# A hybrid decoder step on one core: the sample rows' last tile laid over 128 partitions, and two steps of the ending reordered

## The chip, the cores and the metric

The kernel runs on one core of a Trainium2 chip. The metric is the device time in microseconds of one execution of the whole program, as the median of several runs; a profile of one execution gives the trace that is read here.

## What is computed

One layer of a decoder for 512 prompt rows and 64 sample rows of 1024 values (D), all in float32. The layer is a sum of three gated branches (a state space scan, windowed attention, attention into memory tokens), and then a mixture of experts over all 576 rows. Only its last part matters for this change:

```python
x = x + merged @ lp['w_out']                                  # h
x = x + hier_moe(rmsnorm(x, lp['norm2_g']), lp)               # y = h + w0 * expert_a(x) + w1 * expert_b(x)
...
def rmsnorm(x, g):
    xf = x * lax.rsqrt(jnp.mean(x * x, axis=-1, keepdims=True) + EPS)
    return xf * g
```

Each row goes through two of 32 experts. Its result is h plus the two experts' rows, each times a weight, and the final RMSNorm is taken of that sum with the gain `final_norm_g`.

## The kernel before, in words

The 576 rows lie as five tiles. `WROWS = [64, 128, 128, 128, 128]` and `WTOK = [512, 0, 128, 256, 384]` say that tile 0 holds the 64 sample rows (512 to 575) on 64 partitions, and tiles 1 to 4 hold 128 prompt rows each. Each tile has h in SBUF at `H_AT[t]` as rows of 1024 columns.

The experts' stage runs over 16 pairs of experts (`pairs`). Its weights come in 96 chunks of 1 MB on SyncE's DMA queue (L567), and they are what the stage waits for. The experts' result rows are scattered to a DRAM tensor `expert_rows` by GpSimd (L2929), pair by pair. The last pair's result isn't scattered: it is picked out of PSUM by matmuls with one-hot matrices (`picked`, L1338), after it was split into a high and a low half in fp32r (`L_HI` and `L_LO`, written at L1881 and L2742).

SyncE sets the loads' order around the end (L603 to L617). When the last pair's rows are turned, it issues `load_gain` (L604: the gain, one DRAM row of 4 KB sent to all 128 partitions), which stands in the DMA queue behind the experts' last weights. It then waits for the scatters and issues `load_results` (L609), five loads of `expert_rows` in the order `LOADED = [1, 3, 4, 2, 0]`, 1 MB for each full tile and 512 KB for tile 0.

The ending is written out by hand, the same for TensorE, ScalarE, VectorE and SyncE:

- VectorE adds the first expert's rows to h (`add_first`, L2732), and for tiles 1, 3 and 4 puts that sum plus the second expert's rows into PSUM (`seed`, L2737). Tile 2 gets its second expert's rows in `combine` (L2789), which reads TensorE's sum from PSUM and writes to SBUF. `finish` (L2799, L2800) takes the reciprocal of the root and scales the sum by it and by the gain.
- TensorE (`sums`, L1367) writes a zero first matmul into each seeded PSUM pair (`opening`), adds h of tiles 0 and 2 (`own_rows`), adds the last pair's rows (`picked`), and for tiles 2 and 0 also the loaded rows times their weights (`rows_of`). PSUM holds tile 3's sum in pair ps0, tile 1's and then tile 4's in ps1, tile 2's in ps2 and tile 0's in ps3.
- ScalarE (L1886 to L1893) squares each sum with an accumulated row sum, and takes the root of it.
- SyncE (L634 to L637) stores each finished tile to `out_y`.

```python
ORDER = [1, 3, 2, 0, 4]          # finish and store
...
seed(1); seed(3); add_first(4)
finish(1)
finish(3)
combine(2)
seed(4)
finish(2)
finish(0)
finish(4)
```

(The calls stand one below the other from L2802 to L2811.) Semaphore `more_ps` counts the finished sums in PSUM, `rootf` the roots, `y_done` the finished tiles, `opened` and `seeded` the seeded tiles. The profile's lines L667 and L681 are the helpers through which every matmul and transpose goes.

## Time and profile before

| | |
|---|---|
| median of 3 runs | 781.47 us (778.28 to 782.59) |
| the profiled execution's own time | 779.59 us |
| its span, first to last instruction | 777.8 us |
| granted TensorE clock, mean | 0.993 of full speed |
| busy: TensorE matmul / VectorE / ScalarE / GpSimd | 95% / 53% / 33% / 10% of the span |
| DMA, mean over the span | 245 GB/s |
| last VectorE instruction begins, its length | 771.83 us, 1.28 us |

The profiled execution's own time is 1.79 us longer than its span: what lies around the first and last instruction. Starts in the rows are microseconds from the span's start, so the change's place, the ending, is the stretch from some 728 us on. "Idle before, releaser" says how long an engine stood still before an instruction and what ended that. Time from issue to landing is that of one DMA, from its issue until its semaphore shows it complete.

### The profile page before, as it was taken

What the parts mean: (1) busy time and instruction counts of PE and PEld (TensorE: products, weight loads), DVE (VectorE), ACT (ScalarE), POOL (GpSimd) and SP (SyncE); (2) the same over time, 40 slices, a digit from 0 to 9 for tenths busy, and PEclk for the clock granted to TensorE, in tenths of its full rate; (3) what the DMA queues carried; (4) which work ended last, traced back from release to release, by engine and by line L of the source; (5) the groups of instructions that cost most, each with busy time, mean ns of one, the idle gap of its engine ahead of it and who ended that gap; (6) DMA issues with size and microseconds to landing.
All of it is one profiled execution on the core that took longest, in us unless ns stands there. A gap on an engine that the chain in (4) does not pass through costs nothing.

```text
span 777.8 us, 12795 instructions
## 1 busy us (share of the span) xinstructions
PE 736.3 (95%) x5298; PEld 568.6 (73%) x5298; DVE 409.2 (53%) x756; ACT 260.4 (33%) x451; POOL 74.7 (10%) x105
## 2 busy tenths in 40 slices
PE   8999999999999999999999999998899999778784
PEld 6999999999999777899999988884333333323232
DVE  6999839986347785666154286555121111114226
ACT  5662361123486645443342333230111111100113
POOL 0100022001002111000000100011112212111100
PEclk9999999999999999999999999999999999999998
DMA  9678226434238442500251596389999999999995
GB/s 343 214 271 311 103 82 107 118 116 149 105 120 309 173 158 95 208 1 2 109 184 47 188 413 248 99 354 392 406 422 423 419 423 424 420 425 424 422 395 190
DMA packets 38191, 190.78 MB, mean 245 GB/s; under 512 B 5930, under 2 KB 7498, under 8 KB 21912
## 3 DMA queue, kind: packets, MB, share of 16 engines
q1 hardware_dynamic: 23696, 148.22, 48.3%
q0 software_dynamic: 11248, 35.08, 13.5%
q10 hardware_dynamic: 3184, 6.60, 2.3%
q8 instruction: 44, 0.72, 0.4%
q14 instruction: 19, 0.16, 0.0%
HBM read 176.27 MB, written 21.41 MB: 254 GB/s over the span
## 4 chain that ended last, share of the span: by engine, by line
PE 75%; DMA 15%; DVE 5%; ACT 3%; issue 1%; SPq 1%; ACTq 0%; DVEq 0%; POOLq 0%
PE ps L667 71%; DMA sb<-in_wexp 11%; PE ps L681 4%; DMA expert_rows<-sb 2%; DMA sb<-in_xT 1%; DMA sb<-expert_rows 1%; DVE sb L2800 1%; DVE sb L2330 1%; DVE sb L2316 1%; SPq L567 1%; ACT sb L1455 1%; ACT sb L1655 1%; DVE sb L2732 0%; ACT sb L1677 0%; ACT sb L1660 0%
## 5 line engine op out<-in xcount | busy, mean ns | idle before, releaser
L667 PE MATMUL ps<-sr 128*128 128x288 f32 (+3 forms) x2906 | 407.5, 300 | 2.7 <-DVE ps L2737 2.3
L667 PEld LDWEIGHTS ps<-sr 128*128 128x128 f32 (+1 forms) x2906 | 386.8, 188 | 18.3 <-issue 5.8
L667 PE MATMUL ps<-sb 128*64 128x512 f32 (+17 forms) x1994 | 292.2, 427 | 27.0 <-DMA sb<-in_wexp 15.0
L667 PEld LDWEIGHTS ps<-sb 128*64 128x64 f32 (+7 forms) x1994 | 141.9, 145 | 149.8 <-issue 123.0
L2666 DVE SCALAR_TENSOR_TENSOR sb<-sb,ps 128x256 f32<-128x256 f32 x16 | 6.7, 421 | 116.2 <-ACT sb L1860 116.2
L681 PEld LDWEIGHTS ps<-sb 128*128 128x128 f32 (+3 forms) x398 | 42.2, 140 | 32.6 <-issue 30.2
L681 PE MATMUL ps<-sb 128*128 128x128 f32 (+3 forms) x398 | 53.8, 273 | 3.8 <-DVE sb L2669 1.6
L2278 DVE TENSOR_TENSOR sr<-sb,sr 128x2048 fp32r<-128x2048 f32 (+1 forms) x17 | 39.3, 2319 | 29.0 <-ACT sr L1569 19.0
L2674 DVE COPY sb<-ps 128x1024 f32<-128x1024 f32 x15 | 18.4, 1225 | 57.2 <-PE ps L667 57.2
L1455 ACT ACTIVATE sb<-ps 128x576 f32<-128x576 f32 (+4 forms) x33 | 23.2, 704 | 71.8 <-PE ps L667 56.0
L2389 DVE SCALAR_TENSOR_TENSOR sb<-sb,ps 128x576 f32<-128x576 f32 x24 | 18.1, 752 | 46.5 <-PE ps L667 46.3
L1855 ACT ACTIVATE sb<-ps 128x256 f32<-128x256 f32 x16 | 6.1, 384 | 97.2 <-PE ps L681 97.2
L1860 ACT ACTIVATE sb<-ps 128x256 f32<-128x256 f32 x16 | 6.1, 384 | 78.4 <-PE ps L667 78.4
L1569 ACT ACTIVATE sr<-sb 128x2048 fp32r<-128x2048 f32 x16 | 30.5, 1914 | 1.9 <-ACT sb L1716 0.9
L2929 POOL DMA_INDIRECT expert_rows<-sb x15 | 15.1, 1008 | 154.3 <-DVE sb L2674 139.5
L1716 ACT ACTIVATE sb<-ps 128x288 f32<-128x288 f32 x24 | 9.7, 410 | 54.2 <-PE ps L667 53.8
L2236 DVE TENSOR_TENSOR sr<-sb,sr 128x2048 fp32r<-128x2048 f32 x7 | 16.0, 2292 | 22.5 <-ACT sr L1574 16.6
L2033 DVE TENSOR_TENSOR sr<-sb,sr 128x2048 fp32r<-128x2048 f32 x10 | 22.8, 2292 | 2.3 <-ACT sr L1477 2.0
L1655 ACT ACTIVATE sb<-sb 128x256 f32<-128x256 f32 (+2 forms) x36 | 16.6, 463 | 18.5 <-DVE sb L2333 18.5
L1477 ACT ACTIVATE sr<-sb 128x2048 fp32r<-128x2048 f32 x10 | 19.0, 1911 | 5.1 <-DVE sb L2101 4.5
L1850 ACT ACTIVATE sb<-ps 128x1024 f32<-128x1024 f32 x15 | 15.4, 1024 | 15.3 <-PE ps L681 15.3
L2920 POOL DMA_INDIRECT sb<-xn_rows,sb x15 | 15.3, 1019 | 31.6 <-issue 12.6
(293 smaller groups left out, 499.7 us busy)
## 6 DMA issues: line engine op xcount, KB each, us to landing
sb<-in_wexp SPq DMA_DIRECT2D x91, 1024.0 KB, 21.4
sb<-in_wstream SPq DMA_DIRECT2D x33, 1024.0 KB, 5.5
expert_rows<-sb ACTq DMA_DIRECT2D x1, 4608.0 KB, 24.8
sb<-in_mkT POOLq DMA_DIRECT2D x8, 512.0 KB, 7.9
sb<-in_mv POOLq DMA_DIRECT2D x8, 512.0 KB, 5.3
sb<-expert_rows SPq DMA_DIRECT2D x4, 1024.0 KB, 9.0
sb<-in_wexp SPq DMA_DIRECT2D x5, 768.0 KB, 21.6
sb<-in_x SPq DMA_DIRECT2D x4, 512.0 KB, 14.0
```

The costliest lines, as they stand in the source:

```text
L667: return signed(nc.tensor.matmul(*a, **kw))
L681: return signed(nc.tensor.transpose(*a))
L1455: c.free(fn(dst, src, ACT.Copy, **kw), job)
L1477: fn(r32(EARLY_HI[b], WB), at(raw_at(b), (1, WB)), ACT.Copy).then_inc(hi_ready, 1)
L1569: fn(r32(high_at(block), 2048), at(raw_at(b), (1, WB)), ACT.Copy).then_inc(hi_ready, 1)
L1655: fn(at(sc + m * 256, (1, keys)), at(sc + m * 256, (1, keys)), ACT.Exp, bias=at(stat(n, 1) + m, (1, 1)), accum_out=at(stat(n, 3) + m, (1, 1)))
L1850: fn(at(M_XGT, (1, 1024)), pat(PS_X, 0, (1, 1024)), ACT.Copy).then_inc(xT_sb, 1)
L2033: v.tensor_tensor(r32(raw_at(b), WB), at(raw_at(b), (1, WB)), r32(EARLY_HI[b], WB).bitcast(F32), ALU.subtract).then_inc(lo_ready, 1)
L2236: v.tensor_tensor(r32(src, 2048), at(src, (1, 2048)), r32(hi, 2048).bitcast(F32), ALU.subtract).then_inc(lo_ready, 1)
L2278: v.tensor_tensor(r32(src, n), at(src, (1, n)), r32(hi, n).bitcast(F32), ALU.subtract).then_inc(lo_ready, 1)
L2389: c.free(v.scalar_tensor_tensor(g2, g2, 1.0, pat(pair(name), 0, (512, 2), (1, TH)), ALU.add, ALU.mult), name)
L2674: v.tensor_copy(at(M_YO + (i % 2) * 1024, (1, 1024)), pat(PS_Y, 0, (1, 1024))).then_inc(y_copied, 1)
```

## The change

Tile 0's sum lies in PSUM as 128 partitions by 512 columns now: columns 0 to 511 of its 64 rows on partitions 0 to 63, and columns 512 to 1023 on partitions 64 to 127 (`half_sum`). What reads or writes it follows:

- `own_rows(0)` and `rows_of(0)` write each half to its own 64 partitions. `picked(0)` writes 128 partitions at once, with a one-hot matrix that is moved by 64 places for the second half; for that `L_SEL` has 704 columns instead of 640, and `pick_slots` one small instruction more.
- ScalarE squares 128x512 instead of 64x1024. A row's sum of squares then lies in two parts on partitions p and p+64, which a one-column matmul with the matrix `L_PAIR` adds (`both_squares`); `L_PAIR` is made by one new VectorE instruction in `weight_diagonals`. The root of tile 0 is taken from PSUM, after tile 4's.
- `load_gain` loads the gain a second time in that layout, by two DMAs of 64 partitions by 512 columns to `L_GF`.
- Tile 0 is stored by two DMAs of 64x512.

The order changes too. Tile 0 is squared before tile 4 as before, but finished and stored after it: `ORDER = [1, 3, 2, 4, 0]`. On VectorE `combine(2)` and `seed(4)` stand ahead of `finish(3)`. On TensorE `rows_of(2)` stands ahead of `picked(0)`.

```diff
-ORDER = [1, 3, 2, 0, 4]
+ORDER = [1, 3, 2, 4, 0]
+L_PAIR, L_GF = 46624, O_XH
...
             def load_gain():
                 sp.dma_start(at(M_GF, (1, D)), bass.AP(rows.tensor, rows.offset + D, [[0, P], [1, D]])).then_inc(ld["gf"], 16)
+                for half in range(2):
+                    sp.dma_start(at(L_GF, (1, 512), p0=64 * half, pn=64),
+                                 bass.AP(rows.tensor, rows.offset + D + half * 512, [[0, 64], [1, 512]])).then_inc(ld["gf"], 16)
...
+                if t == 0:
+                    for half in range(2):
+                        sp.dma_start(out_y[WTOK[t]:WTOK[t] + R, half * 512:half * 512 + 512],
+                                     at(H_AT[t], (1, 512), p0=64 * half, pn=64)).then_inc(y_st, 16)
...
+            def half_sum(t, half):
+
+                if t == 0:
+                    return pat(PICKED[t], 0, (1, 512), p0=64 * half, pn=64)
+                return pat(PICKED[t], half * 512, (1, 512), pn=WROWS[t])
...
-                        last = mm(pat(PICKED[t], half * 512, (1, 512), pn=R), r32(L_SEL + WTOK[t], R),
+                        out = pat(PICKED[0], 0, (1, 512)) if t == 0 else half_sum(t, half)
+                        last = mm(out, r32(L_SEL + WTOK[t] + (64 * half if t == 0 else 0), P),
                                   r32(y + half * 512, 512), start=False, stop=(stop and k == 1))
...
+            def both_squares():
+
+                pe.wait_ge(squares, 2 * TT + 3 + 3)
+                mm(pat(PICKED[0], 512, (1, 1)), at(L_PAIR, (1, 128)), at(R_SS + 8, (1, 1)), start=True, stop=True).then_inc(more_ps, 1)
...
                 picked_on_seed(3)
-                picked(0)
                 pe.wait_ge(diag_w, 2)
                 rows_of(2, R_DG)
+                picked(0)
                 pe.wait_ge(y_done, 1)
                 opening(4)
                 rows_of(0, R_BOTH)
                 picked_on_seed(4)
+                both_squares()
...
+            for n, t in enumerate((1, 3, 2)):
+                final_square(n, t)
+                final_root(t)
+            final_square(3, 0)
+            final_square(4, 4)
+            final_root(4)
+            act.wait_ge(more_ps, TT + 1)
+            final_root(0)
...
             def finish(t):
-                R = WROWS[t]
-                h, ss = at(H_AT[t], (1, D), pn=R), at(R_SS + 8 + t, (1, 1), pn=R)
-                total = h if t == 2 else pat(PICKED[t], 0, (1, D), pn=R)
+                n, gf = (512, L_GF) if t == 0 else (D, M_GF)
+                h, ss = at(H_AT[t], (1, n)), at(R_SS + 8 + t, (1, 1))
+                total = h if t == 2 else pat(PICKED[t], 0, (1, n))
...
             finish(1)
-            finish(3)
             combine(2)
             seed(4)
+            finish(3)
             finish(2)
+            finish(4)
             finish(0)
-            finish(4)
```

How the instructions stand, first TensorE's end of `sums`, before. Names with `sr` are fp32r, with `sb` float32; the four `sr` rows of one tile are a `picked`, two `sr` rows with `y_done` are `opening(4)`, and the `sb` rows are `rows_of`.

```order
L667 MATMUL ps<-sr 128x512 [waits seeded]
L667 MATMUL ps<-sr 128x512 x3
L667 MATMUL ps<-sr 64x512 x4
L667 MATMUL ps<-sb 128x512 [waits ld_row2,diag_w]
L667 MATMUL ps<-sb 128x512
L667 MATMUL ps<-sr 128x512 [waits y_done]
L667 MATMUL ps<-sr 128x512
L667 MATMUL ps<-sb 64x512 [waits ld_row0]
L667 MATMUL ps<-sb 64x512
L667 MATMUL ps<-sr 128x512 [waits seeded]
L667 MATMUL ps<-sr 128x512 x3
```

And the same place in the changed kernel:

```order
L676 MATMUL ps<-sr 128x512 [waits seeded]
L676 MATMUL ps<-sr 128x512 x3
L676 MATMUL ps<-sb 128x512 [waits ld_row2,diag_w]
L676 MATMUL ps<-sb 128x512
L676 MATMUL ps<-sr 128x512 x4
L676 MATMUL ps<-sr 128x512 [waits y_done]
L676 MATMUL ps<-sr 128x512
L676 MATMUL ps<-sb 64x512 [waits ld_row0]
L676 MATMUL ps<-sb 64x512
L676 MATMUL ps<-sr 128x512 [waits seeded]
L676 MATMUL ps<-sr 128x512 x3
L676 MATMUL ps<-sb 128x1 [waits squares]
```

The four matmuls of `picked(0)` moved behind `rows_of(2)`, and a one-column matmul came at the end.

VectorE from the first `finish` on, before (L2799 and L2800 are `finish`, L2789 is `combine(2)`, L2737 is `seed(4)`):

```order
L2800 SCALAR_TENSOR_TENSOR sb<-ps,sb 128x1024 [waits vec_step]
L2799 RECIPROCAL sb<-sb 128x1 [waits rootf]
L2800 SCALAR_TENSOR_TENSOR sb<-ps,sb 128x1024 [waits vec_step]
L2789 SCALAR_TENSOR_TENSOR sb<-sb,ps 128x1024 [waits more_ps,ld_row2]
L2737 SCALAR_TENSOR_TENSOR ps<-sb 128x1024 [waits opened]
L2799 RECIPROCAL sb<-sb 128x1 [waits rootf]
L2800 SCALAR_TENSOR_TENSOR sb<-sb 128x1024 [waits vec_step]
L2799 RECIPROCAL sb<-sb 64x1 [waits rootf]
L2800 SCALAR_TENSOR_TENSOR sb<-ps,sb 64x1024 [waits vec_step]
L2799 RECIPROCAL sb<-sb 128x1 [waits rootf]
L2800 SCALAR_TENSOR_TENSOR sb<-ps,sb 128x1024 [waits vec_step]
```

And in the changed kernel:

```order
L2837 SCALAR_TENSOR_TENSOR sb<-ps,sb 128x1024 [waits vec_step]
L2826 SCALAR_TENSOR_TENSOR sb<-sb,ps 128x1024 [waits more_ps,ld_row2]
L2774 SCALAR_TENSOR_TENSOR ps<-sb 128x1024 [waits opened]
L2836 RECIPROCAL sb<-sb 128x1 [waits rootf]
L2837 SCALAR_TENSOR_TENSOR sb<-ps,sb 128x1024 [waits vec_step]
L2836 RECIPROCAL sb<-sb 128x1 [waits rootf]
L2837 SCALAR_TENSOR_TENSOR sb<-sb 128x1024 [waits vec_step]
L2836 RECIPROCAL sb<-sb 128x1 [waits rootf]
L2837 SCALAR_TENSOR_TENSOR sb<-ps,sb 128x1024 [waits vec_step]
L2836 RECIPROCAL sb<-sb 128x1 [waits rootf]
L2837 SCALAR_TENSOR_TENSOR sb<-ps,sb 128x512 [waits vec_step]
```

`combine(2)` and `seed(4)` moved ahead of the second `finish`, and the last instruction works on 512 columns instead of 1024.

SyncE's queue in the changed kernel, from the gain's load on:

```order
L605 DMA sb<-in_rows 128x1024 [waits xt_ps]
L607 DMA sb<-in_rows 64x512 x2
L613 DMA sb<-expert_rows 128x2048 [waits ew_used,y_sent1,y_sent0]
L613 DMA sb<-expert_rows 128x2048 x3
L613 DMA sb<-expert_rows 128x1024
L622 UNCONDITIONAL_BRANCH
L646 DMA out_y<-sb 128x1024 [waits y_done] x4
L643 DMA out_y<-sb 64x512 [waits y_done]
L643 DMA out_y<-sb 64x512
```

The two loads at L607 are new and stand between the gain and the result rows; the last store is two of 64x512 where a 128x1024 one was last.

## Rows read from the trace of the kernel before

**Rows 1.** The page: DMA share in 40 slices of the span; chain shares by engine.
```profile
DMA  9678226434238442500251596389999999999995
...
PE 75%; DMA 15%; DVE 5%; ACT 3%; issue 1%; SPq 1%; ACTq 0%; DVEq 0%; POOLq 0%
```

**Rows 2.** The chain that ended last, 730 to 778 us: start, us, what.
```profile
748.50 5.96 DMA sb<-expert_rows
...
754.49 1.30 DVE sb L2732
...
771.83 1.28 DVE sb L2800
```

**Rows 3.** SyncE's queue in order of time: start, us spent issuing, line, count.
```profile
727.96 1.41 SPq L604 DMA_DIRECT2D sb<-in_rows  x1
748.50 2.62 SPq L609 DMA_DIRECT2D sb<-expert_rows  x5
...
773.14 0.34 SPq L637 DMA_DIRECT2D out_y<-sb  x1
```

**Rows 4.** DMA issues in windows around them: count, KB each, us to landing.
```profile
sb<-in_rows SPq DMA_DIRECT2D x1, 512.0 KB, 24.0
...
sb<-expert_rows SPq DMA_DIRECT2D x1, 1024.0 KB, 6.0
...
sb<-expert_rows SPq DMA_DIRECT2D x1, 1024.0 KB, 12.1
...
out_y<-sb SPq DMA_DIRECT2D x1, 512.0 KB, 2.6
...
out_y<-sb SPq DMA_DIRECT2D x1, 512.0 KB, 4.2
```

**Rows 5.** Packets of a queue in five windows: 62-66, 749.2-749.8, 765.6-768.3, 772.7-774.0, 751.0-751.6.
```profile
q10 hardware_dynamic: 799, 1.64, 104.9%
...
q1 hardware_dynamic: 29, 0.16, 131.9%
...
q1 hardware_dynamic: 275, 1.05, 96.4%
...
q1 hardware_dynamic: 61, 0.25, 90.6%
...
DMA packets 35, 0.26 MB, mean 430 GB/s; under 512 B 2, under 2 KB 2, under 8 KB 5
```

**Rows 6.** Timeline of the ending, VectorE.
```profile
755.81 1.41 DVE L2742 SCALAR_TENSOR_TENSOR sr<-ps,sb,sr 128x512 fp32r<-128x512 f32 x2
...
764.84 1.28 DVE L2800 SCALAR_TENSOR_TENSOR sb<-ps,sb 128x1024 f32<-128x1024 f32 x1
...
766.04 1.27 DVE L2789 SCALAR_TENSOR_TENSOR sb<-sb,ps 128x1024 f32<-128x1024 f32 x1
...
767.23 1.28 DVE L2737 SCALAR_TENSOR_TENSOR ps<-sb 128x1024 f32<-128x1024 f32 x1
...
770.44 1.27 DVE L2800 SCALAR_TENSOR_TENSOR sb<-ps,sb 64x1024 f32<-64x1024 f32 x1
```

**Rows 7.** Timeline of the ending, TensorE; fp32 matmuls leave two records each.
```profile
753.75 1.03 PE L667 MATMUL ps<-sb 128*64 128x512 f32 x4
...
763.63 1.88 PE L667 MATMUL ps<-sb 128*128 128x512 f32 x4
764.94 1.03 PE L667 MATMUL ps<-sr 128*128 128x512 f32 x2
765.90 1.93 PE L667 MATMUL ps<-sb 128*64 128x512 f32 x4
768.57 1.19 PE L667 MATMUL ps<-sr 128*128 128x512 f32 x4 [0.74 <-DVE ps L2737]
```

**Rows 8.** Timeline of the ending, ScalarE: tile 4's square and root.
```profile
770.06 1.00 ACT L1891 ACTIVATE sb<-ps 128x1024 f32<-128x1024 f32 x1
...
771.19 0.29 ACT L1893 ACTIVATE sb<-sb 128x1 f32<-128x1 f32 x1
```

More of the change, by code:

```diff
@@ L1283, in own_rows @@
                 for half in range(2):
-                    mm(pat(PICKED[t], half * 512, (1, 512), pn=R), at(O_ID, (1, R), pn=R),
+                    mm(half_sum(t, half), at(O_ID, (1, R), pn=R),
                        at(H_AT[t] + half * 512, (1, 512), pn=R), start=start, stop=not start)
@@ L1362, in rows_of @@
                 for half in range(2):
-                    last = mm(pat(PICKED[t], half * 512, (1, 512), pn=R), at(weights, (1, R)), at(A_WG[t] + half * 512, (1, 512)),
+                    last = mm(half_sum(t, half), at(weights, (1, R)), at(A_WG[t] + half * 512, (1, 512)),
                               start=False, stop=True)
                 last.then_inc(more_ps, 1)
+            def both_squares():
+                pe.wait_ge(squares, 2 * TT + 3 + 3)
+                mm(pat(PICKED[0], 512, (1, 1)), at(L_PAIR, (1, 128)), at(R_SS + 8, (1, 1)), start=True, stop=True).then_inc(more_ps, 1)
             def sums():
@@ L1885, in _, with final_square, final_root @@
             fn(at(R_SS + 15, (1, 1)), at(O_EPS, (1, 1)), ACT.Sqrt)
-            for n, t in enumerate(ORDER):
-                R = WROWS[t]
-                ss = at(R_SS + 8 + t, (1, 1), pn=R)
+            def final_square(n, t):
+                n_p, n_d = (P, 512) if t == 0 else (WROWS[t], D)
                 act.wait_ge(*((y_sum, 1) if t == 2 else (more_ps, SUMMED.index(t) + 1)))
-                total = at(H_AT[t], (1, D), pn=R) if t == 2 else pat(PICKED[t], 0, (1, D), pn=R)
-                fn(at(M_JUNK, (1, D), pn=R), total, ACT.Square, accum_out=ss).then_inc(squares, 1)
+                total = at(H_AT[t], (1, D)) if t == 2 else pat(PICKED[t], 0, (1, n_d), pn=n_p)
+                fn(at(M_JUNK, (1, n_d), pn=n_p), total, ACT.Square, accum_out=at(R_SS + 8 + t, (1, 1), pn=n_p)).then_inc(squares, 1)
                 act.wait_ge(squares, 2 * TT + 3 + n)
-                fn(ss, ss, ACT.Sqrt, scale=1.0 / D, bias=at(O_EPS, (1, 1), pn=R)).then_inc(rootf, 1)
+            def final_root(t):
+                ss = at(R_SS + 8 + t, (1, 1))
+                total = pat(PICKED[t], 512, (1, 1)) if t == 0 else ss
+                fn(ss, total, ACT.Sqrt, scale=1.0 / D, bias=at(O_EPS, (1, 1))).then_inc(rootf, 1)
+            for n, t in enumerate((1, 3, 2)):
[6 more added lines that the diff above has]
+            final_root(0)
         @block.vector
@@ L2681, in weight_diagonals @@
                 c.settle()
+                op(v.tensor_tensor(at(L_PAIR, (64, 2), (1, 64)), at(O_ID, (0, 2), (1, 64)), at(O_ID + 64, (0, 2), (1, 64)), ALU.add))
                 dve.sem_inc(diag_w, 1)
@@ L2706, in pick_slots @@
                 op(v.tensor_copy(at(L_W + 1, (1, 1)), at(M_IDX + 32 + NPAIR - 1, (1, 1)).bitcast(U32)), False)
+                op(v.tensor_scalar(at(L_TMP + 10, (1, 1)), at(R_IOTA + 8, (1, 1)), -float(RB), None, ALU.mult), False)
                 op(v.tensor_scalar(at(L_TMP, (1, 10)), at(R_IOTA, (1, 10)), -float(RB), None, ALU.mult))
-                op(v.tensor_scalar(at(L_TMP, (1, 10)), at(L_TMP, (1, 10)), at(L_W + 1, (1, 1)), None, ALU.add))
+                op(v.tensor_scalar(at(L_TMP, (1, 11)), at(L_TMP, (1, 11)), at(L_W + 1, (1, 1)), None, ALU.add))
                 dve.wait_ge(xt_ps, NPAIR)
-                c.do(v.tensor_tensor(view(sr, L_SEL, ((RB, 10), (1, RB))), at(R_IOTA, (0, 10), (1, RB)),
-                                     at(L_TMP, (1, 10), (0, RB)), ALU.is_equal), slot_oh, 3)
+                c.do(v.tensor_tensor(view(sr, L_SEL, ((RB, 11), (1, RB))), at(R_IOTA, (0, 11), (1, RB)),
+                                     at(L_TMP, (1, 11), (0, RB)), ALU.is_equal), slot_oh, 3)
             def pairs(i0, i1):
@@ L2774, in _ @@
                 dve.wait_ge(y_sent[1], 16 * (NPAIR_ALL // 2))
-                for dst, n in ((L_HI, 1024), (L_LO, 1024), (L_SEL, 640)):
+                for dst, n in ((L_HI, 1024), (L_LO, 1024), (L_SEL, 704)):
                     v.memset(r32(dst, n).bitcast(F32), 0.0).then_inc(y_lo, 1)
-                dve.wait_ge(ld["gf"], 32)
+                dve.wait_ge(ld["gf"], 96)
                 for t in range(TT):
```

12 lines of the change are left out of this document (6 added, 6 removed).

## The prediction

> **What bounds the kernel now.** I read the page first. TensorE heads the chain with 75%, and the DMA engines are 90% busy or more through the last quarter of the program [rows 1]. The change touches neither the experts' matmuls nor their weights, so the question is what hangs on the ending. The chain of waits over the last 50 us says how the ending is strung: SyncE issues the result loads at 748.50, the first lands 5.96 us later, VectorE starts at 754.49, and from there it is nearly all VectorE up to its last `finish`, 771.83 to 773.11 [rows 2]. Thus two things set the end: when the first result rows land, and how long VectorE's row of seven-odd large instructions takes. Each costs about 1.28 us and follows the one before almost at once [rows 6]. Behind VectorE stands the last store: issued at 773.14 [rows 3], landed 4.2 us later [rows 4], and 777.8 is the end of the span.
>
> **The gain's extra loads: on the path.** SyncE issues `load_gain` at 727.96 [rows 3], and it lands 24.0 us later, at 752.0 [rows 4]. That is after the result loads were issued, and both use the same queue. A load is complete when its slowest DMA engine is done, and in the window from 751.0 to 751.6 there are still 3 packets (5 under 8 KB, 2 of them semaphore writes under 512 B) of the gain's 4 KB kind among the result loads' 8 KB ones [rows 5]. So the slowest engine goes from the gain straight to the first result rows, which land at 748.50 + 6.0 = 754.5, where VectorE waits for them [rows 2, 4]. What is put between the two is added on that engine. The change puts two loads of 64 rows of 2 KB there: 128 packets, 8 on each of 16 engines. The nearest 2 KB packets are those of the queue between 62 and 66 us: 799 packets took 104.9% of 16 engines for 4 us, 84 ns each [rows 5]. 8 x 84 ns = **+0.67 us**. The lower bound is 0, if the slowest engine were not the one that counts. The upper bound of the usual kind is twice the price, 1.35 us, from tile 0's store: 61 packets of 4 KB took 90.6% of 16 engines for 1.3 us, 309 ns each, where the 128-row stores' 256 packets took 96.4% for 2.7 us, 163 ns each [rows 5]. A transfer that touches only 64 partitions went at about half the rate. The upper end of all is 3.5 us, from the slow packets between 749.2 and 749.8: 29 in 131.9% of 0.6 us, 437 ns each, 8 x 437 = 3.5 [rows 5]. I take 0.67, because at 751 the late engine works nearly alone, and because the 2 KB rows are of the same queue kind.
>
> The Trainium skill, "DMA: Bandwidth & Descriptors", section "The descriptor swizzle", says that partitions 0 to 63 lie on the even eight of the 16 SBUF ports and 64 to 127 on the odd eight; its "Rules for kernel authors" say of two transfers to disjoint partition halves: "Don't bother — they serialize". That speaks against the halves here, and tile 0's store at half rate agrees. By that rule the extra loads would cost the 1.35.
>
> All later loads shift with the first, and VectorE's chain with them, so the rest is reckoned in the times of before.
>
> **VectorE's order: earlier by a little.** Before, `finish(3)` starts at 764.84 and `combine(2)` at 766.04 [rows 6]. In the change `combine(2)` can start when `finish(1)` is through, at 764.65 to 764.84, if tile 2's sum is there. The sum: `rows_of(2)` runs 763.63 for 1.88 [rows 7], and four picks go from ahead of it to behind; four such matmuls take 1.19 [rows 7], so it ends at 765.51 - 1.19 = 764.3. Tile 2's loaded rows land 12.1 us after an issue at about 749.8, at 761.9, in time [rows 4]. So `combine(2)` ends near 765.95. `seed(4)` needs `opening(4)`, which stands behind the moved picks: 764.3 + 1.19 + 0.5 to 1.03 [rows 7] = 766.0 to 766.5. That is a new wait of up to 0.6 us on VectorE; `finish(3)`, whose root is long done, is queued behind it, and ScalarE's square of tile 4 waits at its far end. `seed(4)` starts at 766.3 instead of 767.23 [rows 6], ends at 767.6, and the four picks end at 768.8.
>
> Meanwhile `rows_of(0)` runs on TensorE from 766.3. It takes 1.93 if its halves go one after the other, as now, and about 1.03 if they overlap, as four records to alternating halves of the columns do at 753.75 [rows 7]. That puts tile 0's sum at 767.3 to 768.2. The Trainium skill, "TensorEngine Tiling (Array Packing)", section "Key Properties", says that tiles of different columns run in parallel; by it the 1.03 would hold. ScalarE squares 512 columns, between half of 1.00 and all of it [rows 8], with the accumulator's read say 0.8, and is free for tile 4 at 768.2 to 769.0. Tile 4's square and root take 771.19 + 0.29 - 770.06 = 1.42 [rows 8]: the root is there at 770.3 to 770.8. `finish(4)` then runs 770.5 to 771.0 for 1.28, its end 771.8 to 772.3. Tile 0's root follows tile 4's by some 0.3 and is covered by `finish(4)`; the one-column matmul in `both_squares` is covered by tile 4's square. `finish(0)` on 512 columns takes 0.70 (1.41 for two of that size) instead of 1.27 [rows 6] and a reciprocal 0.1. VectorE ends at 772.6 to 773.05 against 773.11: **-0.3 us** (-0.55 to -0.05). It is less than the halved `finish` and the moved steps suggest, since tile 4's path through TensorE and ScalarE is late next.
>
> **The stores: the small gain is spent.** A 512 KB store lands 2.6 us after its issue when nothing is late [rows 4]; by that, before would have been complete at 773.14 + 2.6 = 775.75. Now tile 4's store is issued at about 772.05 and would land at 774.65. Tile 0's two are issued at 772.9 and, after one issue of 0.34 [rows 3], 773.2, so their packets queue behind tile 4's. Their 128 packets of 2 KB, each half on 64 partitions, I price at half the 309 ns of tile 0's 4 KB packets: 8 x 155 ns = 1.24 us [rows 5]. That gives 775.9: the -0.3 of VectorE is spent, and ending and stores together make **+0.15 us**, between -0.5 (2 KB packets at 84 ns, 0.67 instead of 1.24) and +0.4 (VectorE at its late bound). One thing more: the last store took 4.2 us where another of its size took 2.6 [rows 4]. That 1.6 us may stay or go; I keep it, and let its loss be part of the low end.
>
> **Costed at nothing.** The `L_PAIR` instruction, the larger `L_SEL` and the extra instruction in `pick_slots` run beside the last pairs of experts, under weights that keep the DMA engines busy at 90% or more [rows 1]; without that cover they would cost some 0.5 us. GpSimd's queue isn't passed.
>
> **The sum.** +0.67 + 0.15 = +0.8 us. Against the profiled execution: 779.6 + 0.8 = 780.4. That one stood 1.9 us under the median of 781.5. On the median: **782.3 us**. 0.5%, about what a measurement of this kernel can tell from no change, is 3.9 us.
>
> **The rivals.**
> - *The queue has room.* Engines that ended early have a gap between 748.5 and 750; if the extra packets fall into it and the late engine comes no later, +0.67 goes, the ending gains its 0.5, and with the 1.6 us of the last store gone it is -2.1: 779.4 us. For it: the DMA engines move less in that gap. Against it: the engine that is late at 751 has none. 0.25. Still within 0.5%.
> - *Slower.* The gain's halves are read from one DRAM row by all engines while the result loads start, and each packet takes what packets took at 749.2, 437 ns [rows 5]: +3.5, with +0.4 at the end, +3.9, 785.4 us. It decides from 0.43 us per packet on; the late engine's packets must be slow, and not the first ones of the others. 0.05.
> - *The reordering does nothing.* If tile 2's sum or `opening(4)` is later than reckoned by 0.6, VectorE ends at 773.2, and the stores come on top: two issues of 0.34 and 2.6 of landing less the smaller size give at most +0.4, in all +0.67 + 0.4 = +1.1, 782.6 us. 0.15.
> - *The scatter of runs.* Three runs of before lie 4.3 us apart, so a median may seem faster by over 3.9 without a cause: 0.04.
>
> **How the numbers follow.** The forecast has 0.51. Its own bounds are 781.5 - 0.5 and + 1.35 + 0.4, 781.0 to 783.2. The range takes in the first and third rival and half a microsecond of scatter, 778.9 to 784.0; only the slow rival and odd medians lie outside. Faster: 0.04. Slower: the slow rival and scatter, 0.06. Within 0.5%: 0.90.
>
> **What would show it.** In the changed profile the gain's two halves land after 752, and the first result load lands 6.5 to 7 us after its issue instead of 6.0; VectorE's first add begins that much later. From that add to VectorE's last instruction it is 0.1 to 0.6 us less than the 18.6 of before. `combine(2)` follows `finish(1)` without a wait, and `seed(4)` waits 0.2 to 0.6. The chain ends on VectorE and two stores, with the last landing about 2.6 us or more after its issue. I am wrong if the first load lands after 6.0 us again, or if VectorE's ending is more than 1 us shorter.

## The result: slower by 0.29%, and the profile after

| | before | after |
|---|---|---|
| median of the runs (before: all those made beside the change) | 780.71 us | 782.57 us (781.14 to 784.26, 22 runs) |
| ratio after / before | | 1.0029, 95% interval 1.0021 to 1.0036 |
| the profiled execution's own time; its span | 779.59; 777.8 us | 783.69; 781.8 us |
| granted TensorE clock, mean | 0.993 | 0.985 |
| first `add_first` begins | 754.49 us | 757.40 us |
| last VectorE instruction ends | 773.11 us | 777.63 us |

0.29% of 780.7 is 2.3 us. This text goes by the recorded ratios and their intervals; two medians divided by each other can differ from them by up to 0.07% (here 1.0024, 1.9 us). The forecast was +0.8 us (782.3 on the median, range 778.9 to 784.0), no change that can be told. The time is in the range and the difference is under 0.5%, but it is two to three times as large as forecast, and its interval excludes both no change and +0.8. So the question is which term was too small.

The page of after, DMA shares and the chain's shares, against [rows 1]:

```profile
DMA  9578326434238432500260595389999999999993
...
PE 79%; DMA 12%; DVE 5%; ACT 3%; issue 1%; SPq 0%; ACTq 0%; DVEq 0%
```

Nothing has moved there: the ending is 4% of the span. The chain of waits after, last 57 us (start, us, what), against [rows 2]:

```profile
725.85 26.68 DMA sb<-in_wexp
752.52 0.14 issue
752.66 6.57 PE ps L676 x16
...
763.99 7.14 PE ps L676 x18
...
771.16 1.30 DVE ps L2774
...
776.88 0.75 DVE sb L2837
```

Before, this chain went through the first result load. Here it goes through the experts' last weights, which are complete only at 752.5, and then through TensorE. SyncE's queue after (start, us spent issuing, line, count), against [rows 3]:

```profile
728.57 1.40 SPq L605 DMA_DIRECT2D sb<-in_rows  x1
730.01 2.31 SPq L607 DMA_DIRECT2D sb<-in_rows  x2
748.18 3.22 SPq L613 DMA_DIRECT2D sb<-expert_rows  x5
...
777.66 1.40 SPq L643 DMA_DIRECT2D out_y<-sb  x2
```

The two small loads cost SyncE 2.31 us of issuing, under cover of the weights. The result loads are issued no later than before, 748.18 against 748.50. Their landings after (KB each, median us from issue to landing), against [rows 4]:

```profile
sb<-in_rows SPq DMA_DIRECT2D x1, 512.0 KB, 22.0
sb<-in_rows SPq DMA_DIRECT2D x2, 128.0 KB, 22.7
...
sb<-expert_rows SPq DMA_DIRECT2D x4, 1024.0 KB, 12.2
```

VectorE's timeline after (start, us, line, tiles, count, idle before and what ended it), against [rows 6]:

```profile
757.40 1.28 DVE L2769 SCALAR_TENSOR_TENSOR sb<-sb 128x1024 f32<-128x1024 f32 x1 [6.80 <-DMA sb<-expert_rows]
...
759.97 0.75 DVE L2779 SCALAR_TENSOR_TENSOR sr<-ps,sb,sr 128x512 fp32r<-128x512 f32 x1 [0.50 <-ACT sr L1902]
...
766.95 1.28 DVE L2837 SCALAR_TENSOR_TENSOR sb<-ps,sb 128x1024 f32<-128x1024 f32 x1
769.84 1.28 DVE L2826 SCALAR_TENSOR_TENSOR sb<-sb,ps 128x1024 f32<-128x1024 f32 x1 [1.60 <-PE ps L676]
771.16 1.29 DVE L2774 SCALAR_TENSOR_TENSOR ps<-sb 128x1024 f32<-128x1024 f32 x1
...
776.88 0.75 DVE L2837 SCALAR_TENSOR_TENSOR sb<-ps,sb 128x512 f32<-128x512 f32 x1
```

Two things went another way than forecast. The first result load landed 757.40 - 748.18 = 9.2 us after its issue, not 6.5 to 7. And the stretch from that add to VectorE's end is 20.2 us, not 18.0 to 18.5, because VectorE waited 0.50 for ScalarE, which stood behind the last pair's matmuls, and `combine(2)` waited 1.60 for TensorE. The timeline of TensorE and the granted clock after tell why. First the timeline, one line of before and two of after, against [rows 7]:

```profile
751.13 3.65 PE L667 MATMUL ps<-sb 128*64 128x512 f32 x16 [0.47 <-ACT sb L1855]
```
```profile
752.66 6.55 PE L676 MATMUL ps<-sb 128*64 128x512 f32 x16 [1.55 <-DMA sb<-in_wexp]
...
766.93 2.80 PE L676 MATMUL ps<-sb 128*128 128x512 f32 x4
```

Then windows of after (us from:to, length, busy us and count of PE, PEld, DVE, ACT, POOL; granted clock; DMA share; GB/s):

```profile
750.00:751.00 1.00, 0.30 (x2) 0.20 (x2) 0.56 (x2) 0.00 (x0) 0.00 (x0) 1.00 0.90 250
751.00:752.00 1.00, 0.11 (x2) 0.00 (x0) 0.00 (x0) 0.38 (x1) 0.00 (x0) 0.86 1.10 281
752.00:753.00 1.00, 0.34 (x2) 0.32 (x4) 0.00 (x0) 0.00 (x0) 0.00 (x0) 0.50 0.97 281
...
766.00:768.00 2.00, 2.00 (x5) 1.21 (x4) 1.53 (x3) 1.46 (x4) 0.00 (x0) 0.50 0.00 0
```

The last pair's 16 matmuls took 6.55 us here, where the same 16 took 3.65 before, and `rows_of(2)` took 2.80 instead of 1.88 [rows 7], both at the granted clock of 0.50, which is the 1.2 GHz level. The second fall of the clock is in this execution alone of the three profiles of the changed kernel; the other two have 18.1 and 18.0 us for the same stretch (below). So the 20.2 isn't what the change does as a rule, and this profile, 1.1 us above its kernel's median, shows more than the median lost. The other thing is in the last two columns: from 750 to 753 the DMA engines are busy (0.90 to 1.10) and move only 250 to 281 GB/s. Before, one microsecond was as slow, from 749 on (229 GB/s at 0.96), and engines as busy moved 434 to 438 from 751 on:

```profile
751.00:752.00 1.00, 0.87 (x4) 0.34 (x6) 0.00 (x0) 0.07 (x1) 0.00 (x0) 1.00 1.04 438
752.00:753.00 1.00, 1.00 (x8) 0.39 (x6) 0.00 (x0) 0.00 (x0) 0.00 (x0) 1.00 1.04 434
```

A packet is the piece that one DMA engine moves at a time, here 2 to 8 KB of a row. The packets of the 6 us from 748 to 754, before and after (packets, MB, share of 16 engines):

```profile
q1 hardware_dynamic: 331, 2.08, 90.2%
```
```profile
q1 hardware_dynamic: 437, 1.88, 101.9%
```

2.08 MB in 0.902 x 6 us of all engines are 384 GB/s for engines that are fully busy; after, 1.88 / (1.019 x 6) = 307 GB/s. The transfers didn't only become more. They became slower.

### The profile page after: what moved, and what is told of

Its sections match the earlier page's. It is cut to its first block, busy times and chain, and to the rows that moved or that the text cites. A ratio compares the mean times of both kernels' runs of the same rounds, so it can differ in the third digit from the quotient of the medians.

```text
span 781.8 us, 12805 instructions
## 1 busy us (share of the span) xinstructions
PE 738.7 (94%) x5300; PEld 571.3 (73%) x5300; DVE 409.3 (52%) x758; ACT 259.9 (33%) x451; POOL 74.8 (10%) x105
## 4 chain that ended last, share of the span: by engine, by line
PE 79%; DMA 12%; DVE 5%; ACT 3%; issue 1%; SPq 0%; ACTq 0%; DVEq 0%
PE ps L676 75%; DMA sb<-in_wexp 11%; PE ps L690 4%; DMA sb<-in_xT 1%; DVE sb L2365 1%; DVE sb L2351 1%; ACT sb L1476 1%; ACT sb L1676 1%; ACT sb L1698 0%; DVE sb L2729 0%; SPq L568 0%; DVE ps L2774 0%; ACT sb L1681 0%; ACT sr L1743 0%; ACT sb L1871 0%
## 5 line engine op out<-in xcount | busy, mean ns | idle before, releaser
L676 PE MATMUL ps<-sr 128*128 128x288 f32 (+2 forms) x2906 | 408.1, 300 | 2.3 <-DVE ps L2774 1.9
L676 PEld LDWEIGHTS ps<-sr 128*128 128x128 f32 x2906 | 387.3, 188 | 17.9 <-issue 6.3
L676 PEld LDWEIGHTS ps<-sb 128*64 128x64 f32 (+7 forms) x1996 | 144.1, 146 | 151.9 <-issue 125.1
L1676 ACT ACTIVATE sb<-sb 128x256 f32<-128x256 f32 (+2 forms) x36 | 16.6, 463 | 18.6 <-DVE sb L2368 18.5
```

The lines of the kernel that those rows point to most:

```text
L676: return signed(nc.tensor.matmul(*a, **kw))
L1676: fn(at(sc + m * 256, (1, keys)), at(sc + m * 256, (1, keys)), ACT.Exp, bias=at(stat(n, 1) + m, (1, 1)), accum_out=at(stat(n, 3) + m, (1, 1)))
```

## The experiments

The theory: the halves' loads in SyncE's queue cost it all. Rivals were that the new order or the stores cost it, and that the loads cost only their bytes. Four kernels take the change apart. The diffs show the main lines; new semaphores and changed counts are left out (`...`).

**The change without the loads.** GpSimd copies the second layout out of the gain that is there already.

```diff
             def load_gain():
                 sp.dma_start(at(M_GF, (1, D)), ...
-                for half in range(2):
-                    sp.dma_start(at(L_GF, (1, 512), p0=64 * half, pn=64), ...
...
+            for half in range(2):
+                nc.gpsimd.tensor_copy(at(L_GF, (1, 512), p0=64 * half, pn=64),
+                                      at(M_GF + 512 * half, (1, 512), p0=64 * half, pn=64)).then_inc(gf_laid, 1)
```

> The whole change, but the gain's second layout is made on the chip: GpSimd copies 512 columns on partitions 0 to 63 and 512 on 64 to 127 from the gain that is loaded anyway, and the two extra loads go. Theory P (the two 64-row loads disturb the transfers around them: in the changed kernel's trace their 128 packets and the weights and result rows beside them take 1.3 to 1.7 times as long): without them the last weights, the first result rows and TensorE's clock are as before, and only the ending is left. The run is 2 to 4 us faster than the changed kernel, that is 0 to 1.5 us faster than before; first result load lands about 6 us after its issue. Theory Q (they only stand in the queue, 8 packets of 84 ns): 0.7 us faster than the changed kernel and still 1 to 1.5 us slower than before; something in the ending costs the rest.

Measured: 779.77 us, ratio 0.9993 (0.9982 to 1.0005). Against the change, 1.0029 - 0.9993 = 0.36%, 2.8 us. VectorE's timeline of this kernel:

```profile
754.45 1.28 DVE L2766 SCALAR_TENSOR_TENSOR sb<-sb 128x1024 f32<-128x1024 f32 x1 [4.28 <-DMA sb<-expert_rows]
...
763.40 1.28 DVE L2836 SCALAR_TENSOR_TENSOR sb<-ps,sb 128x1024 f32<-128x1024 f32 x1
764.66 1.28 DVE L2823 SCALAR_TENSOR_TENSOR sb<-sb,ps 128x1024 f32<-128x1024 f32 x1
765.96 1.29 DVE L2771 SCALAR_TENSOR_TENSOR ps<-sb 128x1024 f32<-128x1024 f32 x1
...
770.28 1.28 DVE L2836 SCALAR_TENSOR_TENSOR sb<-ps,sb 128x1024 f32<-128x1024 f32 x1
...
771.67 0.75 DVE L2836 SCALAR_TENSOR_TENSOR sb<-ps,sb 128x512 f32<-128x512 f32 x1
```

and its TensorE:

```profile
762.68 1.88 PE L673 MATMUL ps<-sb 128*128 128x512 f32 x4
763.99 1.93 PE L673 MATMUL ps<-sr 128*128 128x512 f32 x6
765.85 1.08 PE L673 MATMUL ps<-sb 128*64 128x512 f32 x4
```

The first add is back where it was before, 754.45 against 754.49 [rows 2], and the ending is clean: 17.97 us from there to 772.42, where before had 18.62. So here the halved `finish` and the new order save 0.65 us; in the three kernels below with the loads behind or tile 0 stored in another way the same stretch is 17.99, 18.37 and 18.23. The median, 0.5 us under before, can't be told from no change, since its interval reaches 1.0005.

**The order alone**, put into the kernel before: `rows_of(2)` ahead of `picked(0)`, and `combine(2)` and `seed(4)` ahead of `finish(3)`.

```diff
-                picked(0)
                 pe.wait_ge(diag_w, 2)
                 rows_of(2, R_DG)
+                picked(0)
...
-            finish(3)
             combine(2)
             seed(4)
+            finish(3)
```

> The kernel before with the reordering alone: combine of tile 2 and seed of tile 4 ahead of finish of tile 3 on VectorE, rows_of(2) ahead of picked(0) on TensorE; tile 0 as it was. By my reckoning VectorE waits for opening(4) and tile 4's path through TensorE and ScalarE is the bound: VectorE ends 0 to 0.6 us earlier, the time is 0 to 0.6 us shorter. The rival: the reordering puts waits on VectorE that it did not have (in the changed kernel combine of tile 2 waits 1.6 us for TensorE) and costs 0.5 to 1 us.

Measured: 780.04 us, 1.0 (0.999 to 1.0009). The order costs nothing that can be told, and by itself brings nothing that can be told.

**The loads alone**, put into the kernel before, where nobody reads them. VectorE's first `finish` waits for them too, as in the change; but their last packet ends at 754.0, and that `finish` comes at 765.95.

```diff
+L_GF = O_XH
...
             def load_gain():
                 sp.dma_start(at(M_GF, (1, D)), ...
+                for half in range(2):
+                    sp.dma_start(at(L_GF, (1, 512), p0=64 * half, pn=64),
+                                 bass.AP(rows.tensor, rows.offset + D + half * 512, [[0, 64], [1, 512]])).then_inc(ld["gf"], 16)
```

> The kernel before with nothing but the two extra loads of 64 rows by 512 columns behind the gain's load; nobody reads what they load. Theory P: 2 to 3.5 us slower than before. Theory Q: 0.7 us slower.

Measured: 783.0 us, 1.003 (1.0018 to 1.0043), +2.3 us. That is the whole of the change's loss, and the change without them had none. The cause is the loads, and not the order, the layout or the stores.

**The same bytes in one load of 128 rows**, also in the kernel before: 128 packets of 2 KB again, all from the first half of the gain.

```diff
+                sp.dma_start(at(L_GF, (1, 512)), bass.AP(rows.tensor, rows.offset + D, [[0, P], [1, 512]])).then_inc(ld["gf"], 16)
```

> The kernel before with one extra load of 128 rows by 512 columns behind the gain's load: the same 256 KB in the same 128 packets of 2 KB from the same DRAM row, but each DMA engine writes the partitions it writes in every 128-row load. If 64 partitions are what disturbs (several engines write to one side of SBUF), this costs the queue's 0.7 us and no packet is slow; if it is the reading of one DRAM row by all engines, or small packets, it costs as much as the two halves, 2 to 3.5 us. Theory Q: 0.7 us, as the halves.

Measured: 781.63 us, 1.0016 (1.0003 to 1.0029), +1.25 us. The packets of the 6 us from 748 to 754, first with the two halves, then with the whole:

```profile
q1 hardware_dynamic: 424, 1.81, 98.3%
```
```profile
q1 hardware_dynamic: 479, 2.23, 97.2%
```

The same bytes of gain, as many packets and the engines as busy, but 2.23 MB against 1.81. The rate of fully busy engines in that window is MB / (share x 6 us). The last column needs no window: it is the time from the issue of the result loads to the first `add_first`, which waits for the first of them.

| kernel | halves loaded ahead of the results | MB, share | GB/s | issue to first add, us |
|---|---|---|---|---|
| before | no | 2.08, 90.2% | 384 | 5.99 |
| order alone | no | 2.02, 88.8% | 379 | 6.52 |
| change without the loads | no | 2.28, 95.3% | 399 | 6.82 |
| one load of 128 rows | no | 2.23, 97.2% | 382 | 7.11 |
| change, loads behind (below) | no | 2.18, 93.9% | 387 | 6.51 |
| two queues (below) | no | 2.17, 93.3% | 388 | 7.07 |
| one store (below) | no | 2.28, 93.1% | 408 | 6.47 |
| the change | yes | 1.88, 101.9% | 307 | 9.22 |
| the change again | yes | 1.93, 100.4% | 320 | 8.65 |
| the change, third profile | yes | 1.90, 93.7% | 338 | 8.21 |
| the loads alone | yes | 1.81, 98.3% | 307 | 8.46 |

With the halves, every kernel lies at 307 to 338; without, at 379 to 408. The two kernels below whose gain's load was moved have 379 and, in a window with its engines only 39.1% busy, 354. Windows of 6 us that begin 1 us ahead of each kernel's own issue of the result loads part them more cleanly: 311 to 320 with the halves, 378 to 408 without. The landings part in the same way: 8.2 to 9.2 us after the issue with the halves, 6.0 to 7.1 without, about 2 us apart.

The records of the single packets (start, duration and size) show the slowing packet by packet. The extra 2 KB packets took 84 ns each in the one load and 102 to 112 in the mean in the four profiles with the halves. The gain's 4 KB packets that began between 750 and 752 took 159 to 178 ns in the mean without the halves and 195 to 235 beside them; the 8 KB packets that began between 752 and 754 took 310 to 327 (355 in one kernel with the gain's load moved) and 413 to 473.

The engines' 1.9 MB of that window take 1.9 MB / 320 - 1.9 MB / 390 = 1.1 us longer, about the difference between the two kernels (2.3 - 1.25). In the times alone that difference is at the edge of noise: the intervals of the two, 1.0018 to 1.0043 and 1.0003 to 1.0029, overlap.

**The change, its loads behind the result loads.** In the same queue, with a semaphore of their own that only `finish(0)` waits for.

```diff
             def load_results():
                 for t in LOADED:
                     ...
+                for half in range(2):
+                    sp.dma_start(at(L_GF, (1, 512), p0=64 * half, pn=64),
+                                 bass.AP(rows.tensor, rows.offset + D + half * 512, [[0, 64], [1, 512]])).then_inc(gf_laid, 16)
```

> The changed kernel with its two extra loads, only issued behind the five result loads instead of ahead of them. They are wanted 8 us later than that. Theory P: the disturbed stretch moves from the path to a place where only tile 0's rows and the first stores are beside it; the first result load lands 6 to 7 us after its issue again, and the kernel is 2 to 2.8 us faster than the changed one, within 0.5 us of the copy on the chip (0.9993 of before). If the loads cost in whatever place they stand (rival), it stays 1 us or more slower than before.

Measured: 780.27 us, 1.0001 (0.9989 to 1.0013). The same two loads, issued at 751.82 instead of 730.01, cost 2.2 us less (1.0029 - 1.0001 = 0.28%). The first add comes 6.51 us after the issue again. So it isn't the loads that are dear but their place ahead of what is waited for. Nothing is won against before.

**Two other ways to store tile 0**, both made from the change without the loads. In the first, half 1 goes from ScalarE's queue:

```diff
-                    for half in range(2):
+                    for half in range(1):
                         sp.dma_start(out_y[WTOK[t]:WTOK[t] + R, half * 512:half * 512 + 512], ...
...
+            act.wait_ge(y_done, TT)
+            act.dma_start(out_y[WTOK[0]:WTOK[0] + 64, 512:1024], at(H_AT[0], (1, 512), p0=64, pn=64)).then_inc(y_st, 16)
```

> The kernel with the gain copied on the chip, and tile 0's second half stored from ScalarE's queue instead of SyncE's, so that the halves are issued together and each DMA engine can turn from one to the other. In the traces the second issue on SyncE took 0.8 and 1.6 us and the packets of 2 KB took 147 ns instead of 84. If both are from one queue sending one half after the other, this saves 0.5 to 1.2 us. If the packets are slow because each transfer touches 64 partitions, whichever queue sends it, only the issue is saved, at most 0.5 us, or nothing.

Measured: 780.49 us, 1.0002 (0.9988 to 1.0016). In the second, one store takes all 128 partitions to 128 consecutive pieces of 2 KB. The halves of the sample rows then lie in another order than they should, so this kernel serves for its time alone:

```diff
-                    for half in range(2):
-                        sp.dma_start(out_y[WTOK[t]:WTOK[t] + R, half * 512:half * 512 + 512], ...
+                    sp.dma_start(out_y[WTOK[t]:WTOK[t] + R, :].rearrange("r (h c) -> (r h) c", h=2),
+                                 at(H_AT[t], (1, 512))).then_inc(y_st, 16)
```

> The kernel with the gain copied on the chip, and tile 0 stored by one DMA of 128 partitions by 2 KB to consecutive addresses (so the sample rows' halves land in another order in the output than the reference has them). Same bytes, same 128 packets, but one issue, and every DMA engine reads the partitions it reads in other stores. Theory P: packets at 84 ns, 8 x 84 = 0.67 us instead of 1.2 to 1.3 for the data, and no second issue: 0.6 to 1.2 us faster than with two stores, that is 1.1 to 1.7 us faster than before. If the last landing hangs on one late DMA engine alone, as tile 4's 4 KB packets suggest, at most 0.3 us.

Measured: 779.85 us, 0.9992 (0.998 to 1.0004). Both are within noise of the kernel they were made from. The last landings (median us from issue), first of the change without the loads, then of the one store, then of the two queues, then of the change itself:

```profile
out_y<-sb SPq DMA_DIRECT2D x2, 128.0 KB, 3.8
```
```profile
out_y<-sb SPq DMA_DIRECT2D x1, 256.0 KB, 4.6
```
```profile
out_y<-sb ACTq DMA_DIRECT2D x1, 128.0 KB, 4.7
```
```profile
out_y<-sb SPq DMA_DIRECT2D x2, 128.0 KB, 3.0
```

However the last store is shaped, its landing comes 3.0 to 4.7 us after the issue, where before had 4.2 for a store of 512 KB [rows 4]. The change's own two halves are at 3.0, but their two issues took SyncE 1.40 us. From VectorE's end to the end of the span it is 4.1 to 5.2 us in all fourteen profiles, 4.7 in before. Neither the size of the store nor that of its packets sets it here.

**The changed kernel again**, for a second profile:

> The changed kernel once more, for a second profile. Theory P: the packets behind the gain's load are slow again (4 KB packets above 159 ns and 2 KB ones above 84 ns around 750 us), and the first result load lands 8 us or more after its issue. If it was an accident of one execution, it lands 6.7 us after. TensorE's clock, which stood at half for 7 us from 751 in the first profile and for 3 at 765, may or may not fall; where it doesn't, VectorE's row from its first add to its last instruction takes 18.0 us, not 20.2.

Measured: 782.4 us in one run; the loads' slow window (table), and 18.14 us from the first add to VectorE's end.

**The gain's first load also moved**, behind the first three result loads: once in the change without the loads, once in the kernel before.

```diff
             def load_results():
                 for t in LOADED:
                     ...
+                    if t == LOADED[2]:
+                        load_gain()
             sp.wait_ge(xt_ps, NPAIR)
-            load_gain()
```

> The kernel with the gain copied on the chip, and the gain's one load (128 rows of 4 KB, 8 packets of 159 ns on each DMA engine) issued behind the result loads of tiles 1, 3 and 4 instead of ahead of all of them. If the slowest DMA engine's row of packets is what sets the first result rows, as the forecast of the extra loads assumed, they land 8 x 159 ns = 1.3 us earlier and so does all behind them: 0.9 to 1.3 us faster than with the gain ahead, 1.4 to 1.8 us faster than before. Rival: the result loads are issued at 748.5 and cannot be there before some 5 us later (fixed cost and the slow first packets of 0.5 to 1.2 us), so only 0 to 0.5 us is won.

> The kernel before with nothing but this move of the gain's load. By the queue theory 0.9 to 1.3 us faster than before, as above; by the rival 0 to 0.5 us. If tile 1's finish now waits for the gain instead, it shows as an idle stretch on VectorE ahead of the first reciprocal, longer than the 0.4 us it has.

Measured: 781.0 us, 1.0002 (0.999 to 1.0014), and 780.56 us, 0.9993 (0.9979 to 1.0007). In the second the first add came at 754.23 instead of 754.49, and VectorE then waited for TensorE and ScalarE:

```profile
754.23 1.28 DVE L2732 SCALAR_TENSOR_TENSOR sb<-sb 128x1024 f32<-128x1024 f32 x1 [3.22 <-DMA sb<-expert_rows]
756.52 0.75 DVE L2742 SCALAR_TENSOR_TENSOR sr<-ps,sb,sr 128x512 fp32r<-128x512 f32 x1 [1.01 <-ACT sr L1881]
```

The first add came 5.61 us after the issue of the result loads (before 5.99) in this kernel, and 4.93 (6.82 in the change without the loads) in the other. So with 512 KB less ahead of them the results do land earlier, but the time shows no gain that can be told (-1.6 to +0.5 us by the second interval). VectorE's waits of 1.01 and 0.81 us hang on the last pair's matmuls, which come no earlier, and took 5.32 us in this profile, at a granted clock of 0.50 to begin with, where before they took 3.65.

**One transfer for both halves**, a mend of the change, with the change beside it on the same chip.

```diff
-                for half in range(2):
-                    sp.dma_start(at(L_GF, (1, 512), p0=64 * half, pn=64),
-                                 bass.AP(rows.tensor, rows.offset + D + half * 512, [[0, 64], [1, 512]])).then_inc(ld["gf"], 16)
+                sp.dma_start(at(L_GF, (1, 512)),
+                             bass.AP(rows.tensor, rows.offset + D, [[512, 2], [0, 64], [1, 512]])).then_inc(ld["gf"], 16)
```

> The changed kernel, but the gain's second layout is loaded by one transfer to 128 partitions (128 rows of 2 KB, two different pieces of the gain) instead of two of 64 partitions. Bytes and packets are the same. Theory A (half of the price is what a transfer to 64 partitions does to the packets): the packets are at 84, 159 and 309 ns again, the window 751 to 754 moves about 436 GB/s less what ends early, the price falls from some 2.3 us to the 1.25 of the whole-row load in the kernel before, and the ratio is 1.0007 to 1.0015. Rival B (the second layout, not the 64 partitions, is what slows them: two pieces of one row read side by side): packets slow as before, ratio 1.0025 to 1.0035. Rival C (with one transfer less, nothing is left of the price): ratio 0.999 to 1.0003.

> The changed kernel itself, on the same chip as the one-transfer kernel, for a direct comparison. Expected: ratio 1.002 to 1.0035 to the kernel before, slow packets (2 KB at 110 to 150 ns) from the halves' start on; under theory A 0.8 to 1.5 us above the one-transfer kernel, under B within 0.4 us of it, under C 2 us or more above it.

Measured: 785.03 us, 1.006 (1.0048 to 1.0073), and 783.1 us, 1.0029 (1.002 to 1.0038) for the change. None of the three theories had that. The mend costs 1.9 us more than what it mends. The landings of the result loads, first with one transfer, then the change beside it:

```profile
sb<-expert_rows SPq DMA_DIRECT2D x4, 1024.0 KB, 14.4
sb<-expert_rows SPq DMA_DIRECT2D x1, 512.0 KB, 17.8
```
```profile
sb<-expert_rows SPq DMA_DIRECT2D x4, 1024.0 KB, 11.2
sb<-expert_rows SPq DMA_DIRECT2D x1, 512.0 KB, 14.5
```

and VectorE's first adds with one transfer:

```profile
759.05 1.28 DVE L2768 SCALAR_TENSOR_TENSOR sb<-sb 128x1024 f32<-128x1024 f32 x1 [8.35 <-DMA sb<-expert_rows]
...
762.28 1.28 DVE L2768 SCALAR_TENSOR_TENSOR sb<-sb 128x1024 f32<-128x1024 f32 x1 [0.49 <-DMA sb<-expert_rows]
```

The records of the single packets say what is different. In the change the 2 KB packets come in runs of 8 one behind the other, from several engines at once, up to seven. With one transfer the first 16 follow each other without a gap, and over the 7.7 us of all 128 there are one or two at a time for 7.25 us. So the transfer ran on about two engines, some 64 packets each, instead of 8 on each of 16: at the 104 ns that they took in the mean, 64 x 0.104 = 6.7 us on an engine that the result rows then had to wait for. The Trainium skill, "DMA: Bandwidth & Descriptors", "Rules for kernel authors", says so: an outermost dimension of size c under 16, "e.g. a leading zero-stride broadcast of c copies", confines the whole DMA to at most c engines. My pattern had an outermost 2, and the trace agrees. The experiment therefore doesn't tell theory A from B: it changed the number of engines too. What it does show is that a transfer to 128 partitions can have slow packets. Its window from 748 to 754 holds

```profile
q1 hardware_dynamic: 400, 1.91, 99.8%
```

which is 1.91 / (0.998 x 6) = 319 GB/s, among the halves' values (332 in a window that begins 1 us ahead of the result loads' issue), and its 2 KB packets took 104 ns and not 84.

**What stays open.** The halves and this transfer have two things in common that the load of 128 rows from one piece of the gain has not: they read two pieces, and their engines may write other partitions than in a full load. Which engine writes what, no trace here shows. The Trainium skill, "DMA: Bandwidth & Descriptors", "The descriptor swizzle", gives each engine one port of its own in a 128-partition transfer, which would fit the second. A load of 64 partitions twice from the same piece, or of 128 from two pieces on 16 engines, would tell them apart. Neither was run.

## Why the prediction was right in its kind and wrong in its size

- **The time itself, 782.3 forecast and 782.57 measured: luck.** The sum was added to the median of three runs, 781.47, and the median of 22 runs of the same kernel is 780.71. The base was 0.8 us too high and the sum 1.1 to 1.5 us too low.
- **What bounds the kernel**, the first landing and VectorE's row: right. Loads that touch no instruction of the ending moved the time by 2.3 us, and the change with the same loads placed some 22 us later is at 1.0001.
- **The gain's extra loads, +0.67 us: the step that failed.** The sentence was 8 x 84 ns, "because at 751 the late engine works nearly alone". It measured +2.3 us (the loads alone), and 2.8 between the change with and without them. The loads' bytes alone, in packets of normal length, cost about 1.25 us (0.2 to 2.3), not resolved from 0.67. What was wrong is that the term counted only the loads' own packets. The change made the packets around them slow as well, the experts' last weights and the result rows, at 307 to 338 GB/s instead of 379 to 408: another 1.1 us by that rate, for which the sum had no term. The 6.5 to 7 us forecast from the result loads' issue to their first landing were 8.2 to 9.2 in the three profiles of the change. That whatever stands ahead adds its packets' time on the slowest engine isn't settled either: the gain's load moved away, 8 x 159 ns = 1.3 us by that rule, brought the first landing 0.4 us nearer to its issue in one kernel and 1.9 in the other. By the Trainium skill's rule on partition halves ("DMA: Bandwidth & Descriptors", "Rules for kernel authors"), named in the prediction, it would have been 1.35, nearer, but a price for the halves alone again.
- **The upper bound** of 3.5 us and the rival "Slower" did hold the right kind of thing, slow packets while the result loads start. Its price, 437 ns, was that of a few packets for the loads' own 8 per engine. In truth packets of all kinds became slower by less, over a longer time. I gave it 0.05, and its point of 0.43 us per packet wasn't reached: the halves' packets took 0.10 to 0.11.
- **VectorE's order, -0.3 us:** right in sign, and a little larger: -0.65 in the change without the loads (17.97 against 18.62), -0.5 and -0.65 in the second and third profiles of the change (18.14 and 17.97). `combine(2)` followed `finish(1)` at once, as forecast, save in the two profiles whose clock fell at `rows_of(2)`. `seed(4)` was to wait 0.2 to 0.6 for `opening(4)`; it didn't. The picks and the opening ended at 763.99 + 1.93 = 765.92 and VectorE began at 765.96: I had put the opening's end at 766.0 to 766.5. `rows_of(0)` took 1.08, so its halves overlap, as taken from the four records to alternating halves; the Trainium skill's "TensorEngine Tiling (Array Packing)", "Key Properties", has tiles of different columns run in parallel, and the trace agrees.
- **Tile 4's path is late next:** right, but by 0.15 us only: `finish(4)` began 1.54 us after `finish(2)` in the change without the loads, where `finish(2)` had begun 1.39 after the one ahead. It began at 770.28 in the clean profile (forecast 770.5 to 771.0), and VectorE ended at 772.42 (772.6 to 773.05).
- **The stores, at half the 309 ns:** a store of halves moved 67 data packets and 16 of the semaphore in 59.7% of 16 engines for 1 us, 0.597 x 16 / 67 = 142 ns each, against 155 taken. The row is that of the change without the loads, 775 to 776:

```profile
q1 hardware_dynamic: 83, 0.15, 59.7%
```

  But the price didn't decide. From VectorE's end to the span's end it was 4.7 us before, 4.2 in the change, 4.9 without the loads and 5.1 with the one whole store; the prediction had kept the 1.6 us over a landing in 2.6, and such a landing came in none of them.
- **L_PAIR and the rest at nothing:** nothing speaks against it. The change without the loads has them all and isn't slower than before.
- **The sum:** +0.8 forecast. By the runs it is +2.3 for the loads (of it 1.25 their bytes) and -0.5 (between -1.4 and +0.4) for all the rest, +1.8 together; the change itself measured +2.3 (1.6 to 2.8).

## What to carry to other kernels

A DMA put ahead of one that is waited for can cost more than its bytes: look for what its packets do to the transfers beside it, and compare MB at a given busy share, not the share alone. A second layout of data that is already on the chip is cheaper as a copy by an idle engine, or as a load behind what is waited for, than as a load ahead of it; here either gave back 2.2 to 2.8 us. And a smaller last instruction bought nothing that could be told here, with 4.1 to 5.2 us from VectorE's end to the end of the span whatever the store's shape.

No version tried beats the kernel before by more than can be told: the lowest ratios are 0.9993 (the change without the loads, and before with the gain's load moved) and 0.9992 (the one whole store, which puts the sample rows' halves in the wrong order), and their intervals reach 1.0004 to 1.0007.

## What the runs showed of the hardware that was not expected

- 256 KB in two loads of 64 partitions lowered what busy DMA engines moved by about a sixth, for 3 to 6 us, the neighbours' transfers included; 256 KB in one load of 128 rows didn't.
- A transfer whose pattern begins with a dimension of two ran on about two engines and made the kernel 1.9 us slower than two transfers on all of them.
- TensorE's granted clock fell to 0.50 around the last pair's matmuls in eight of the thirteen profiles of this study other than that of before, those of kernels without any extra load too. How busy TensorE had been just before doesn't always part them. The 5 us ahead of those matmuls, first in before, where the clock stayed, then in the order alone, where it fell as they began:

```profile
746.13:751.13 5.00, 3.10 (x17) 0.98 (x13) 0.84 (x2) 0.77 (x2) 0.00 (x0) 1.00 0.85 319
```
```profile
748.67:753.67 5.00, 3.10 (x16) 0.98 (x13) 0.84 (x2) 0.77 (x2) 0.00 (x0) 0.99 0.90 329
```

  The last pair's 16 matmuls took 6.55 us at the 1.2 GHz level in the profile of after, and 5.30 in the order alone, where the clock came back before they ended. What that costs depends on when the results land. In the two other profiles of the change and in the loads alone VectorE waited for the result load then, and for nothing more. In the four profiles with such a fall and no halves (order alone, one load of 128 rows, two queues, before with the gain's load moved) VectorE waited 0.96, 0.26, 0.31 and 1.82 us for ScalarE behind those matmuls, and in the profile of after 0.50. A fall at `rows_of(2)` cost more: 1.60 us at `combine(2)` in the profile of after, and 3.49 in the first of the two with the gain's load moved, part of it a wait of 1.07 us for result rows. What sets a fall off in one execution and not in the next stays open.
